# First two up-projection chunks of each FFN from the un-normalised residual, and five adaLN vectors made inside the attention

## What is computed

```python
def _modulate(x, shift, scale):
    return x * (1.0 + scale) + shift
def _swiglu(h, w_in, w_out):
    up, gate = jnp.split(h @ w_in, 2, axis=-1)
    return (jax.nn.silu(gate) * up) @ w_out
...
        ml = [m[:, None, :] for m in jnp.split(sc @ mod_w[l] + mod_b[l], 6, axis=-1)]
...
        x = _layer_norm(ALPHA * x + ml[2] * y_lat, ln_g[l, 0], ln_b[l, 0])
        x = _layer_norm(ALPHA * x + ml[5] * _swiglu(_modulate(x, ml[3], ml[4]), ffn_w_in[l], ffn_w_out[l]),
                        ln_g[l, 1], ln_b[l, 1])
```

## Time and profile before

| | us |
|---|---|
| median of three runs | 1986.89 |
| lowest, highest | 1985.92, 1993.27 |
| profiled execution | 1980.92 |
| its span | 1979.2 |

### The profile page before, as it was taken

One profiled execution on the slowest core, in us unless ns is written; L12 is line 12 of the kernel. 1 busy time (PEld: TensorE's weight loads), 2 busy tenths in 40 slices (PEclk: granted clock), 3 DMA queues, 4 the chain that ended last, 5 costly groups with the idle time before them and its releaser, 6 DMA issues.

```text
span 1979.2 us, 24735 instructions
## 1 busy us (share of the span) xinstructions
PE 1813.5 (92%) x10000; PEld 1455.6 (74%) x10000; DVE 607.9 (31%) x1135; ACT 598.9 (30%) x825; POOL 635.0 (32%) x341
## 2 busy tenths in 40 slices
PE   4999989999896999999999996989767889999996
PEld 2888757577683888888888884777555568888885
DVE  2134244555426111111111136730187431111114
ACT  1532222444325221122111224442233353223124
POOL 0442201000154333222321245433235554434343
PEclk8999989999997999999999997999798989999999
DMA  8421232200326122212221126222103433333221
GB/s 283 116 54 54 64 107 86 86 1 1 108 63 202 54 64 81 61 50 64 75 64 54 48 62 195 66 63 64 43 1 110 140 91 105 103 90 106 85 77 51
DMA packets 210263, 162.80 MB, mean 82 GB/s; under 512 B 17662, under 2 KB 190942, under 8 KB 210182
## 3 DMA queue, kind: packets, MB, share of 16 engines
q1 hardware_dynamic: 207744, 157.77, 26.4%
q10 hardware_dynamic: 2438, 3.90, 0.5%
HBM read 159.55 MB, written 2.10 MB: 82 GB/s over the span
## 4 chain that ended last, share of the span: by engine, by line
PE 79%; DVE 10%; ACT 4%; issue 3%; DMA 2%; POOL 1%; ACTq 0%; DVEq 0%; SPq 0%
PE ps L608 58%; PE ps L596 2%; PE ps L598 2%; PE ps L597 2%; PE ps L812 2%; PE ps L764 2%; PE ps L789 2%; DMA ring<-in_mod_w 2%; PE ps L705 1%; PE ps L721 1%; PE ps L560 1%; DVE xT L1740 1%; DVE xT L1730 1%; PE ps L799 1%; DVE cacc L1831 1%
## 5 line engine op out<-in xcount | busy, mean ns | idle before, releaser
L2063 POOL TENSOR_TENSOR wlo<-ring,whi 128x1024 fp32r<-128x1024 f32 (+1 forms) x136 | 317.7, 2348 | 566.6 <-ACT whi L1318 566.5
L608 PE MATMUL ps<-hlo,whi 128*128 128x512 f32 (+1 forms) x1152 | 347.1, 355 | 0.0
L608 PE MATMUL ps<-hhi,whi 128*128 128x512 f32 (+1 forms) x1056 | 318.3, 356 | 10.8 <-DVE modc L1525 8.7
L608 PE MATMUL ps<-hhi,wlo 128*128 128x512 f32 (+1 forms) x1056 | 317.5, 355 | 0.0
L608 PEld LDWEIGHTS ps<-hlo,whi 128*128 128x128 f32 x1152 | 189.8, 189 | 31.6
L608 PEld LDWEIGHTS ps<-hhi,whi 128*128 128x128 f32 x1056 | 174.1, 189 | 40.5 <-DVE modc L1525 8.8
L608 PEld LDWEIGHTS ps<-hhi,wlo 128*128 128x128 f32 x1056 | 173.9, 189 | 29.6
L1788 DVE TENSOR_TENSOR hu<-sg,ps 128x768 f32<-128x768 f32 (+1 forms) x44 | 36.1, 821 | 503.2 <-ACT sg L1330 503.2
L1318 ACT ACTIVATE whi<-ring 128x1024 fp32r<-128x1024 f32 (+1 forms) x136 | 135.0, 1024 | 175.4 <-PE ps L608 173.5
L1703 DVE SCALAR_TENSOR_TENSOR xT<-ps,modc,xT 128x512 f32<-128x512 f32 x96 | 60.6, 659 | 322.7 <-PE ps L608 214.9
L608 PE MATMUL ps<-uhi,whi 128*128 128x512 f32 (+1 forms) x528 | 158.0, 353 | 0.0
(11 more groups left out here) (289 smaller groups left out, 2674.8 us busy)
## 6 DMA issues: line engine op xcount, KB each, us to landing
ring<-in_mod_w SPq DMA_DIRECT2D x96, 512.0 KB, 5.1
ring<-in_ffn_w_in SPq DMA_DIRECT2D x88, 512.0 KB, 3.8
ring<-in_ffn_w_out SPq DMA_DIRECT2D x32, 512.0 KB, 4.1
ring<-in_m_w_in SPq DMA_DIRECT2D x24, 512.0 KB, 3.7
ring<-in_ab_w_in SPq DMA_DIRECT2D x21, 512.0 KB, 3.9
ring<-in_ffn_w_out SPq DMA_DIRECT2D x16, 384.0 KB, 3.3
ring<-in_ab_w_out SPq DMA_DIRECT2D x8, 512.0 KB, 4.8
ring<-in_m_w_out SPq DMA_DIRECT2D x8, 512.0 KB, 4.8
```

What stands on the lines that cost most here:

```text
L608: mm = pe.matmul(dst[:, a:b], w, h[:, a:b], start=st, stop=sp_)
L2063: pool.tensor_tensor(wlo[:, s, 0:width], ring[:, (NB[f"ffn{l}"] + s) % RING, 0:width], whi[:, s, 0:width].bitcast(F32), ALU.subtract).then ...
```

## The change

**Early tiles.** During the output projection ScalarE writes `zhi` = round(`gain0` x `xT`) and VectorE the rest `zlo`, chunk by chunk, from the residual not yet normalised. Four more columns (two in layer 1) hold -`gain0` and `gain1`. The first four up-projection tiles (two hidden chunks, values and gates) are multiplied from these, so that behind the tokens stand two extra columns, the products of the weights with -`gain0` and `gain1`. The LayerNorm sums follow the first of these tiles. At evacuation (`late_tile` of VectorE) a tile becomes (product + mean x column 1) x `lnr`, and column 2 is added as a bias of the Silu or in the product. In layer 1 512 tokens plus two columns don't fit one bank, so each product is a 256-wide and a 258-wide matmul. Tiles 5 to 8 are made from `hhi`, `hlo` as before. The first four weight tiles of the FFN are split at the end of the output projection; the high and low parts share a new tile `wsplit`, and some tiles are placed anew.

**adaLN vectors.** `mod10`, `mod11`, `mod05`, `mod14` and `mod15` are made in the attention: from step 3 on, each vector takes nine steps, one unit at the end of each of eight steps and the column transposes at the ninth. All four matmuls of a unit write the first 256 columns of `half(7)`, on different partitions. The values of the attention now have `half(6)` alone, and wait for the norm of the step before. `gains` of the two later LayerNorms follow earlier, and the ring's order changes accordingly.

The diff, cut to its core:

```diff
     STAGES = (("mod00", KD), ("mod01", KD), ("in0", N_IN0), ("mod03", KD), ("mod04", KD), ("mod02", KD), ("mod10", KD),
-              ("out0", N_OUT), ("mod11", KD), ("mod05", KD), ("ffn0", N_FFN), ("mod12", KD), ("mod13", KD), ("in1", N_IN1),
-              ("mod14", KD), ("out1", N_OUT), ("mod15", KD), ("ffn1", N_FFN))
+              ("mod11", KD), ("mod05", KD), ("mod14", KD), ("mod15", KD), ("out0", N_OUT), ("ffn0", N_FFN), ("mod12", KD), ("mod13", KD), ("in1", N_IN1),
+              ("out1", N_OUT), ("ffn1", N_FFN))
...
+    LATE_MM = (((0, LAT, 0), (LAT, ZW, 512)), ((0, 256, 0), (256, LAT + 2, 512)))
+    LATE_TOKENS = (((0, LAT, 0, 0), (LAT, T, 512, 1)), ((0, 256, 0, 0), (256, LAT, 512, 0)))
+    LATE_COL = (T, 512 + 256)
+    ATT_MODS, ATT_MOD_FIRST, ATT_MOD_STEP = ((1, 0), (1, 1), (0, 5), (1, 4), (1, 5)), 3, 9
     H_CREDIT = 2
...
     def op_pair(i):
-        return PS[(i + 1) % 4]
+        return PS[i % 4]
+
+    def ln_pairs(i):
+
+        return (PS[0], PS[1]) if i % 2 else (PS[2], PS[3])
...
+        def mod_rows_stacked(l, g, bank, first=0, end=KD):
+
+            for k in range(first, end):
+                n = NB[f"mod{l}{g}"] + k
+                loaded(n)
+                for b in range(4):
+                    mm = pe.matmul(bank[32 * b:32 * b + 2, 0:256], s_kv[:, k, :], ring[:, n % RING, 256 * b:256 * (b + 1)],
                                    start=(k == 0), stop=(k == KD - 1))
                 mm.then_inc(unit_done, 1)
...
-            if it >= 2:
-                pe.wait_ge(att_n, it - 1)
+            if it >= 1:
+                pe.wait_ge(att_n, it)
             else:
                 pe.wait_ge(mod_ev, MOD_AT[0, 2])
             j0 = 0 if t < LT else LT
             for j in range(j0, TT):
-                mm = pe.matmul(half(6 + it % 2)[:, 0:MLA_V], paT[:, it % 2, j * P:(j + 1) * P],
+                mm = pe.matmul(half(6)[:, 0:MLA_V], paT[:, it % 2, j * P:(j + 1) * P],
                                va[:, j, h * MLA_V:(h + 1) * MLA_V], start=(j == j0), stop=(j == TT - 1))
...
-            if i >= N_ATT:
-                q = (i - N_ATT) * 4
-                mod_rows(1, 0, PS[0], q, q + 4)
+            q, k = divmod(i - ATT_MOD_FIRST, ATT_MOD_STEP)
+            if 0 <= q < len(ATT_MODS):
+                if k == 0:
+                    pe.wait_ge(mod_ev, MOD_AT[ATT_MODS[q - 1] if q else (0, 2)])
+                if k < KD:
+                    mod_rows_stacked(*ATT_MODS[q], half(7), k, k + 1)
+                if k == ATT_MOD_STEP - 1:
+                    mod_columns(*ATT_MODS[q], half(7))
...
-                if l == 1 and (c == 0 or c in NORM_ENDS):
-                    pe.wait_ge(mn_done, 1 + (NORM_ENDS.index(c) + 1 if c else 0))
-                if l == 0 and c == 1:
-                    mod_columns(1, 0, PS[0])
-                if l == 1 and c == 1:
+                if l == 1 and c < 2:
+                    pe.wait_ge(mn_done, NP - 1 + c)
+                if l == 1 and c == 2:
                     pe.wait_ge(m_num, LT * NP)
-                if c == (1 if l == 0 else 3):
-                    pe.wait_ge(mod_ev, MOD_AT[1, 4 * l])
+                if l == 0 and c == 3:
+                    pe.wait_ge(mod_ev, MOD_AT[ATT_MODS[-1]])
...
-                    mm = pe.matmul(PS[q][:, a:b], ones, src[:, a:b], start=True, stop=True)
+                    mm = pe.matmul(ln_pairs(i)[q][:, a:b], ones, src[:, a:b], start=True, stop=True)
...
+                def late_tile(s, k):
+                    ws = slice(k * P, (k + 1) * P)
+                    for w, z, st, sp_ in ((0, zhi, k == 0, False), (0, zlo, False, False), (1, zhi, False, k == KD - 1)):
+                        for a, b, at in LATE_MM[l]:
+                            mm = pe.matmul(PS[s][:, at:at + b - a], w_part(s, w)[:, ws], z[:, k, a:b], start=st, stop=sp_)
+                    return mm
                 if third == 0:
-                    pe.wait_ge(h_done, J - 1 + H_CREDIT)
+                    pe.wait_ge(z_cols, l + 1)
+                    for s in range(4):
+                        pe.wait_ge(lo_made, U + s + 1)
+                        if s == 2:
+                            pe.wait_ge(ln_mean, 2 * l + 1)
+                        if s == 3:
+                            pe.wait_ge(ln_var, 2 * l + 1)
+                        for k in range(KD):
+                            if s == 0:
+                                pe.wait_ge(z_lo, KD * l + k + 1)
+                            mm = late_tile(s, k)
+                        mm.then_inc(ffn_tile, 1)
+                        if s == 0:
+                            ln_sums(2 * l)
+                    pe.wait_ge(h_done, J + 1 + H_CREDIT)
...
                                 if ks == 0:
-                                    pe.wait_ge(lo_made, U + s + 1)
+                                    pe.wait_ge(lo_made, U + 4 + s + 1)
...
+                    pe.wait_ge(h_done, J + 2 + H_CREDIT)
                     for s in (2, 3):
-                        if s == 2:
-                            pe.wait_ge(h_done, J + H_CREDIT)
-                        pe.wait_ge(lo_made, U + s + 1)
+                        pe.wait_ge(lo_made, U + 4 + s + 1)
...
-                with pe.Fori(0 if third else 1, nj // 2) as it:
+                with pe.Fori(0 if third else 2, nj // 2) as it:
...
-                            mm = tile(s, k, uhi[:, k, :], ulo[:, k, :], k == nj - 1)
+                            mm = tile(s, k, *hidden(third, k), k == nj - 1)
...
-        ln_with_mod(0, KD, (1, 1), (0, 5))
...
-        mod_rows(1, 4, PS[0])
-        mod_columns(1, 4, PS[0])
...
+        def late_high(l, m):
+            act.wait_ge(z_ev, ZB[l] + m + 1)
+            for a, b, v in SEGS[l]:
+                ins = act.activation(zhi[:, m, a:b], xT[:, m, a:b], ACT.Copy, scale=gain[:, 2 * l, 0, m, v:v + 1])
+            ins.then_inc(z_hi, 1)
...
+                else:
+                    ffn_split_static(l, m + 2 - KD, UNIT)
+                if m == 0:
+                    act.wait_ge(gains_ok, 2 * l + 1)
+                late_high(l, m)
                 ln_square(2 * l, m)
+            act.wait_ge(unit_done, UB[f"out{l}"] + KD)
+            ffn_split_static(l, 2, UNIT)
+            ffn_split_static(l, 3, UNIT)
...
-            from_norm(2 * l, hhi, hlo_raw, lambda v: split_static(v, UNIT))
...
+            def between(k):
+                if k <= 1:
+                    split_static(4 + k, UNIT)
+                if k == 3:
+                    late_silu(0)
+                if k == 5:
+                    late_u(0)
+
+            from_norm(2 * l, hhi, hlo_raw, between)
+            late_silu(1)
+            late_u(1)
...
+            if 0 <= q < len(ATT_MODS) and k == KD - 1:
+                mod_rows_stacked(*ATT_MODS[q], half(7))
+            if 0 <= q < len(ATT_MODS) and k == ATT_MOD_STEP - 1:
+                mod_columns(*ATT_MODS[q], half(7))
+        gains(1)
...
+        def late_low(l, m):
+            dve.wait_ge(z_hi, KD * l + m + 1)
+            for a, b, v in SEGS[l]:
+                ins = dve.scalar_tensor_tensor(zlo[:, m, a:b], xT[:, m, a:b], gain[:, 2 * l, 0, m, v:v + 1],
+                                               zhi[:, m, a:b].bitcast(F32), ALU.mult, ALU.subtract)
+            ins.then_inc(z_lo, 1)
+
+        def late_tile(l, j, g, dst):
+
+            nt, nc_ = NT[l], 2 * (2 - l)
+            step(dve.tensor_copy(late_c[:, j, g, 0:nc_], PS[2 * j + g][:, LATE_COL[l]:LATE_COL[l] + nc_]))
+            for a, b, at, v in LATE_TOKENS[l]:
+                ins = dve.scalar_tensor_tensor(dst[:, a:b], lnm[:, a:b], late_c[:, j, g, 2 * v:2 * v + 1],
+                                               PS[2 * j + g][:, at:at + b - a], ALU.mult, ALU.add)
+            step(ins)
+            return dve.tensor_tensor(dst[:, 0:nt], dst[:, 0:nt], lnr[:, 0:nt], ALU.mult)
+
+        def late_gates(l, j):
+            dve.wait_ge(ffn_tile, FT[l] + 2 * j + 2 + TILE_CREDIT)
+            late_tile(l, j, 1, sg[:, j, :]).then_inc(late_gate, 1)
+
+        def late_values(l, j):
+            dve.wait_ge(uhi_done, JB[l] + j - 1 + U_CREDIT)
+            step(late_tile(l, j, 0, hu[:, j, :]))
+
+        def late_product(l, j):
+            dve.wait_ge(silu_done, JB[l] + j + 1)
+            for a, b, v in SEGS[l]:
+                ins = dve.scalar_tensor_tensor(hu[:, j, a:b], hu[:, j, a:b], late_c[:, j, 0, 2 * v + 1:2 * v + 2], sg[:, j, a:b],
+                                               ALU.add, ALU.mult)
+            ins.then_inc(h_done, 1)
+
+        def late_rest(l, j):
+            nt, (hi, lo) = NT[l], hidden(0, j)
+            dve.wait_ge(uhi_done, JB[l] + j + 1 + U_CREDIT)
+            dve.tensor_tensor(lo[:, 0:nt], hu[:, j, 0:nt], hi[:, 0:nt].bitcast(F32), ALU.subtract).then_inc(ulo_done, 1)
...
                 dve.wait_ge(xa_done, KD * 2 * l + m + 1)
                 z_update(l, 2, m, op_pair(m))
                 if m >= 1:
+                    late_low(l, m - 1)
                     ln_sum(2 * l, m - 1, ZB[l] + m)
```

(6 more changed lines are left out.)

120 lines of the change are left out of this document (79 added, 41 removed).

## The result

The changed kernel takes 1957.2 us (median of 4 runs, 1951.4 to 1961.0) where the kernel before took 1986.4 (4 runs, 1983.4 to 1993.3) beside it: ratio 0.9836, 95% interval 0.9802 to 0.9870. That is 29.2 us less; 37.2 were predicted, and the 1957.2 lie in the range 1930 to 1974. The profiled executions took 1980.92 and 1957.35, only 23.6 apart. Much of what follows is about why these three differences are not the same.

A forecast was written before the change was run, and what follows sets the result against it. TensorE, busy 92% of the span, was taken to bound the kernel. Savings of 31.3 + 17.6 + 11.3 + 5, less 28 in the attention, make 37.2 us: 1986.9 to 1950 us, range 1930 to 1974, likeliest 1938 to 1962.

The forecast's parts named there:

- gap of layer 0: Layer 0, between output projection and FFN: early tiles remove 37.0 us, less 3.2 for sums and 2.5 waits, saving 31.3.
- gap of layer 1: Layer 1, same place: 27.1 us less 2.2 sums, 1.3 narrower matmuls and 6.0 waits, saving 17.6.
- `mod10` ahead of projection 0: Before layer 0's output projection: without the `mod10` matmuls the projection starts earlier, 11.3 us saved.
- `mod14` ahead of projection 1: Before layer 1's output projection: without `mod14` only six small gain operations stay in between, 5 us saved.
- attention: Attention: 40 adaLN units at 0.70 us plus 4.5 for columns, less 4.6 of covered waits, net +28 us.
- some 5 us, while TensorE works through six chunks for 6.2: Start of the early tiles: the last two chunks are ready in 5 us, before TensorE finishes six, so no wait.
- No clock is lost, since the engine stops nowhere: Start of the early tiles in layer 0: TensorE runs on from the projection, so the 2.5 us clock loss goes.
- The added unit gives it 0.7 us more room: Attention: with one value bank, values wait for the previous step's norm, which gains 0.7 us from the added unit.
- Units in bubbles: Rival, attention: units fit into TensorE's waits, so it grows by only +14 us; 1936 us in all, chance 0.16.
- Longer waits: Rival, behind early tiles: GpSimd meetings stop TensorE 6 to 10 us twice, plus 2.4 clock per layer; 1974, chance 0.13.
- Early tiles late: Rival, output projection: `zlo` comes late, shifting the tiles some 15 us per layer; saved 7, 1980, chance 0.05.
- Four matmuls in a row: Rival, attention: a unit's four matmuls in one bank run one after another, 1.44 us more each; 2008, chance 0.05.

The follow-up runs named there:

- e11: A variant of the changed kernel with early tiles and TensorE's two stops still there; the text does not say which edit or time; gap of layer 0 42.3 us.
- e1: The changed kernel run once more, unchanged; median 1963.5 us, ratio 0.984 to the kernel before.
- e9: The changed kernel with two GpSimd waits: layer 1 output weight splits after the gain operations, third and fourth up-projection splits after the last LayerNorm sum; 1951.8 us, ratio 0.980.
- the pairs run: The changed kernel with the attention's adaLN units two at a time in every second step instead of one per step; 1959.0 us, ratio 0.9872.
- e4: The kernel before with only the five adaLN vectors moved into the attention, no early tiles; 1995.6 us against 1990.1, ratio 1.0018.

## Why the prediction was right, and where not

Direction and range held, and so did the two mechanisms, the early tiles directly behind the projection and the vectors in the attention. Of the signs named in advance three failed: the clock did fall below 1.00, the wait for `wsplit` in layer 1 did not come, and the projection of layer 1 came hardly any earlier. The term of each step (us), read from the first two profiles:

| term | predicted | measured |
|---|---|---|
| gap of layer 0 | -31.3 | -24.8 |
| gap of layer 1 | -17.6 | -16.8 |
| `mod10` ahead of projection 0 | -11.3 | -8.9 |
| `mod14` ahead of projection 1 | -5.0 | -0.6 |
| attention | +28.0 | +21.7 |
| sum | -37.2 | -29.4 |

- **Gap of layer 0, mis-sized by 6.5.** I had 37.0 less 3.2 (sums) less 2.5 (waits). The rows: waits 0.8 + 1.7 + 2.6 = 5.1; sums 4.3, since TensorE stopped ahead of them; the tiles 43.6 - 5.1 - 4.3 = 34.2 instead of 33.2, of which 0.6 is the slower pace (96 pairs) and not the change's; and 1.8 at a lower clock behind the stop (16.0 less 81 records of 0.1757, above). The clock's part is this execution's: in e11, with the same stops at full clock, the gap of 42.3 and nothing lost behind it make the term -28. The failed step is "some 5 us, while TensorE works through six chunks for 6.2": it took VectorE's two low halves at 1.14 and left out the splits for tiles 3 and 4, queued on GpSimd in just that stretch. I had counted two meetings, both later. "No clock is lost, since the engine stops nowhere" was said of the start of the tiles, but stood beside a sum with stops of 2.0 and 0.5 in layer 0 and of 3.1 and 2.9 in layer 1, for which no clock was counted either.
- **Gap of layer 1, right in size, by luck.** Waits 5.2 (6.0), sums 2.0 (2.2), narrower matmuls 1.3 (1.3), and again 1.8 of clock that I had not: 27.1 - 10.3 = 16.8. It came out by two errors that cancel: the wait for the seventh weight (2.9) did not come, the one ahead of the sums (1.5) and the clock did. Other executions lost more behind this stop (e1: clock 0.60 over 7.6 us instead of 0.78).
- **`mod10`, 2.4 less than said.** The last values began at 532.6, the projection at 541.1, 8.5 later (from the start of their last matmul, as in the table above, 8.2; in other traces of the changed kernel up to 9.2), where I had 7.3 made of estimated short steps; the rest is that I had moved the last values themselves forward by 1.15 under this term, and they now stand in the attention's.
- **`mod14`, the term that failed.** I filled the stretch with "six small gain operations, taken as 2 us" and asked nothing of GpSimd. The rule that I had quoted for the other gap, and the question which transfer starts earlier when `mod14` no longer holds the ring, give the answer together. e9 got 3.9 of it back. (The table's two traces differ by 0.6; the other traces of the changed kernel had 19.6, 1.5 less than before.)
- **Attention, 6.3 too dear.** The gross price was fair: from the start of the transposes to that of the scores it is 477.00 - 475.69 = 1.31, where a step of the kernel before had 0.66 (480.14 to 480.80), and the scores take 478.39 - 477.00 = 1.39 instead of 1.30, so a unit costs 0.74 (I had 0.70), and columns, whose steps are 0.04 longer, 0.78. What I mis-sized is the cover: 4.6 us of listed waits, while 40 x 0.74 + 5 x 0.78 = 33.5 gave only 21.7. Two of six steps in a head are set by the single bank and take a unit for nothing, and the rest of TensorE's slack was in no row of waits. "The added unit gives it 0.7 us more room" was right for full steps; without units the bank costs 17.81 - 16.58 less six tiny matmuls of 0.14, that is 0.4 us a head (the steps of the pairs run that hold no unit add up to 17.01, the same 0.4).
- **The rivals.** Units in bubbles (+14): part of it happened, 21.7 lies midway. Longer waits: the stops came to 5.1 and 5.2 plus 1.8 each, not the 6 to 10 twice. Early tiles late: no, they began 0.1 us behind the projection. Four matmuls in a row: refuted.
- **The difference of 6 us** between the profiled execution of before and the median, "for which no row gives a cause": the profile had caught the quicker pace, and its repetition at the slower one took 1991.7. That the pace alone makes the 6 us is argued, not shown: the other runs have no trace, and e4's 1997.6 at the quicker pace shows another cause at work.

By terms 29.4, by medians 29.2; that they agree so closely is luck, with single times spread over 10 us on both sides. The 23.6 of the two profiles is 29.4, less 9.8 for the slower pace in layer 0's FFN, plus 2.7 for two faster projections, plus the 2.2 ahead of the attention, less 1.4 in the rest: 23.1, which leaves 0.5 of rounding.

## What to carry to other kernels

When a change removes work ahead of a stage, list what was queued behind that work on every engine, weight splits above all, and place it in the new timeline: here GpSimd's splits moved onto VectorE's critical steps and took back 3 to 4 us in each of two places, until a wait put them into VectorE's idle time. Before comparing two profiles, compare the matmul count of a stretch where nothing waits, and the granted clock behind each stop; two executions of one kernel differed by 10 us by the first and by 1 to 3 by the second, and a term of a few us must be read from its own stage.

## What was not expected of the hardware

- Alternating matmuls of 512 and 256 columns run at one of two steady paces, 579 or 567 to 569 records in 100 us, at a granted clock of 1.00; one program, the kernel before, shows both in different executions. Two other orders of the same matmuls gave 574 and 571, and their four times each lay within 3.4 and 2.4 us.
- A VectorE operation on 128x8 elements in SBUF took 2.26 and 2.31 us beside a GpSimd split, 0.16 without.
- Four fp32 matmuls on four column groups into one bank took 0.61 us, one alone 0.60.
- What a stop of TensorE costs behind it differs between executions: after a stop of 2.1 to 2.9 us in layer 0 the granted clock over the next 7.6 us was 1.00 in five traces and 0.78 to 0.81 in six, 1.8 us lost at 0.78; after 3.7 us in layer 1 it was 0.78 in the changed kernel and 0.60 in its repetition.
